# One stage for the front of block 1: projection, convolution, decay and scan on a ring of weight slabs

## The chip, the cores and the metric

The kernel runs on one core of a Trainium2 chip. It is one launch, and its time is the device time of that launch in microseconds. Of the core's engines, TensorE (PE in the profile) multiplies, with its weight loads shown apart (PEld); VectorE (DVE), ScalarE (ACT) and GpSimd (POOL) work element by element; SyncE (SP) issues the DMAs. Each engine takes its instructions strictly in the order in which they are written, and waits on semaphores where an operand comes from another engine.

## What is computed

Two blocks of two layers each work on a sequence of 512 positions and 1024 channels in float32. The change touches the front of block 1:

```
h = rms_norm(x, g_mix[i])
(a_q, a_k, a_v, s_z, s_x, s_b, s_c, s_dtf, s_dtb,
 c_q, c_k, c_v, d_uv) = jnp.split(h @ w_in[i], offsets, axis=-1)        # 2824 columns
...
xbc = jax.nn.silu(depthwise_conv_centred(jnp.concatenate([xs, bm, cm], axis=-1), conv_w, conv_b))
delta_f = jax.nn.softplus(dt_f.astype(f32) + dtb_f.astype(f32))
y_f = ssd_chunked(xh, delta_f, -jnp.exp(alog_f.astype(f32)), bg, cg)
y_b = jnp.flip(ssd_chunked(jnp.flip(xh, 1), jnp.flip(delta_b, 1), ...), 1)
y = (y_f + y_b + d_skip[:, None] * xh).reshape(b, s, d_x) * jax.nn.silu(z)
return rms_norm(y, g_norm)
```

`ssd_chunked` is a scan in four chunks of 128 positions, for four heads and in two directions: cumulated decays, their exponentials (`decay_in`), the products of C and B within a chunk (here "gram"), a state per chunk (`chunk_states`), the states carried from chunk to chunk, and the outputs. Behind the front stand two attentions, a spatial gate, the branch gates and `w_out`, then a mixture of experts and a gated side input.

## The kernel before

A product "exact" in float32 is made of three fast ones: both operands are split into a high part (ScalarE rounds it, `ring_hi`, `W_hi`, `T_hi`) and a low part (VectorE subtracts, `ring_lo`, `W_lo`, `T_lo`), and TensorE adds hi x hi, lo x hi and hi x lo. Every weight therefore passes DMA, ScalarE and VectorE before TensorE can use it. A float32 product without the split stands in the program once and in the trace as two records.

A layer of block 1 is a row of stages. Each is one `nc.Block()`: all engines meet at its end.

- `norm_stage`: norms the residual `X`, transposes it, and leaves `T_hi` and `T_lo`, channels on the partitions. With `save` it also writes `X` to DRAM (2 MB). Its parameter `slabs` (block 2 uses it) loads three weight slabs and splits the first.
- `project_stage`: 2824 columns in six chunks of 472, each for four token tiles and in two halves of the contraction, 24 products a tile, 576 in all. A half chunk of weights is loaded when `lo_ready` says its buffer is split. ScalarE and VectorE evict into `Z`, tokens on the partitions. The skewed bias table is written meanwhile.
- `conv_stage`: transposes the x, B and C channels to have channels on the partitions (24 transposes), convolves over five taps (VectorE, L544 and L549), applies silu with a sigmoid table, and transposes four tiles back (16).
- `decay_stage`: softplus, cumulative sums by products with triangular matrices (L601, L602), `spread` tiles (L629), their column sums over all partitions (L607), the differences (L641), exponentials (ScalarE, L592), and a product on GpSimd (L614).
- `scan_stage`: gram products (L687), diagonal outputs (L693), states (L697), `prev` carried by VectorE (L745 to L751), outputs (L706), gate and norm (L758 to L778).
- `late_stage`: 32 gate tiles, the two attentions and `w_out`, in an order that `steps` and `order` write out. Gate weights come in slabs of 1 MB through a ring of three (`ring_land`): slab q + 3 is requested when the last step of slab q is done (`load_slab`), then split by `to_hi` and `to_lo`. Four `turn` steps (j == 8 and j == 10) transpose the second attention's q and k tiles out of `Z` into `QK`.

The order on every engine is the order of the code; there is no scheduler.

## Time and profile before

| | |
|---|---|
| median of 3 runs | 4164.09 us (4161.66 to 4168.14) |
| the profiled execution | 4161.74 us, its span 4160.0 us |
| mean granted TensorE clock | 0.936 of full speed |
| busy: PE, DVE, ACT, POOL | 3607.9, 1716.3, 1080.5, 24.3 us |
| DMA | 644.75 MB, mean 155 GB/s |

How to read it: the span runs from the first to the last instruction; the rest of an execution's time lies around it. Shares of the whole span mix stages with different limits, so the change is read from the stages it touches. A row of the timeline is a run of like instructions: start, length, engine, line, operation, names of what is written and read, and in brackets how long the engine had been idle and whose work ended that. Overlapping TensorE records have modelled ends: the distance of starts tells their pace. In a stretch's row, "PEclk" is the granted clock, 1.00 being 2.4 GHz and 0.50 being 1.2 GHz.

### The profile page before, as it was taken

The numbers are of one execution on the slowest core, as the hardware profiler recorded it, in microseconds if no ns is written. First come the engines' busy times: TensorE is split into PE (matmuls) and PEld (weight loads), VectorE is DVE, ScalarE is ACT, GpSimd is POOL, SyncE is SP. The second block draws the span as 40 slices with busy tenths as digits, with TensorE's granted clock in tenths as the row PEclk, the third lists the DMA queues.
The fourth block names the chain that finished last, engine by engine and source line by source line (L and its number), as shares of the span: only waits on it lengthen the run. The fifth ranks groups of instructions, "written<-read, shape, count | busy, mean of one in ns | idle before, by whom it ended". The sixth has DMA issues, their size and how long they took to land. (4 is left out here: it accounts for less than half of the span.)

```text
span 4160.0 us, 45410 instructions
## 1 busy us (share of the span) xinstructions
PE 3607.9 (87%) x17600; PEld 2423.6 (58%) x17600; DVE 1716.3 (41%) x3020; ACT 1080.5 (26%) x1655; POOL 24.3 (1%) x34
## 2 busy tenths in 40 slices
PE   7669996999988679996999975989899869898998
PEld 6546675444457456674444453756666746566666
DVE  2475643212133565643221232347643323486433
ACT  3233321100123223321101033333332133323321
POOL 0010000000000000000000000000000000000000
PEclk9879998999998879998999998989999989899999
DMA  3121125999923121125999914111112241111122
GB/s 134 49 89 51 64 89 210 423 424 424 423 91 114 40 98 55 51 89 244 423 424 423 423 67 192 61 41 51 58 70 76 95 174 61 41 51 66 61 76 102
DMA packets 128280, 644.75 MB, mean 155 GB/s; under 512 B 19749, under 2 KB 42277, under 8 KB 61785
## 3 DMA queue, kind: packets, MB, share of 16 engines
q1 hardware_dynamic: 128088, 642.17, 39.3%
q8 instruction: 124, 2.03, 0.2%
q14 instruction: 68, 0.55, 0.0%
HBM read 631.61 MB, written 14.70 MB: 155 GB/s over the span
## 5 line engine op out<-in xcount | busy, mean ns | idle before, releaser
L1463 PE MATMUL ps<-normed_T_hi,ring_split 128*128 128x512 f32 (+1 forms) x1952 | 638.0, 409 | 42.1 <-PEq L268 15.6
L1463 PEld LDWEIGHTS ps<-normed_T_hi,ring_split 128*128 128x128 f32 (+1 forms) x1952 | 369.5, 193 | 155.1 <-issue 45.8
L1463 PE MATMUL ps<-normed_T_lo,ring_split 128*128 128x512 f32 (+1 forms) x976 | 387.7, 397 | 0.0
L2112 PE MATMUL ps<-normed_T_hi,ring_split 128*128 128x512 f32 x1024 | 338.1, 412 | 18.1 <-DVE branches L2371 16.1
L1739 DVE TENSOR_TENSOR ring_split<-weight_ring,ring_split 128x2048 fp32r<-128x2048 f32 x76 | 174.0, 2290 | 300.9 <-ACT ring_split L1624 300.9
L2112 PEld LDWEIGHTS ps<-normed_T_hi,ring_split 128*128 128x128 f32 x1024 | 194.1, 193 | 89.9 <-issue 29.7
L257 PE MATMUL ps<-weights_hi,normed_T_hi 128*128 128x472 f32 (+1 forms) x512 | 199.0, 389 | 32.2 <-DVE weights_lo L361 23.3
L1463 PEld LDWEIGHTS ps<-normed_T_lo,ring_split 128*128 128x128 f32 (+1 forms) x976 | 187.4, 192 | 42.4
L2112 PE MATMUL ps<-normed_T_lo,ring_split 128*128 128x512 f32 x512 | 203.5, 397 | 0.0
L257 PE MATMUL ps<-weights_lo,normed_T_hi 128*128 128x472 f32 (+1 forms) x512 | 197.6, 386 | 0.0
L257 PE MATMUL ps<-weights_hi,normed_T_lo 128*128 128x472 f32 (+1 forms) x512 | 196.4, 384 | 0.0
L1519 PE MATMUL ps<-branches 128*128 128x512 f32 x384 | 173.0, 593 | 1.6 <-DVE work L1813 1.6
L1036 PE MATMUL ps<-weight_ring,projected 128*64 128x512 f32 x768 | 167.9, 593 | 0.0
L1624 ACT ACTIVATE ring_split<-weight_ring 128x2048 fp32r<-128x2048 f32 x76 | 144.7, 1907 | 36.3 <-DMA weight_ring<-in_w_slabs 28.2
L2155 PE MATMUL ps<-branches,rope_tables_T 128*128 128x512 f32 x256 | 121.3, 596 | 9.4 <-DVE work L2356 5.2
L1014 PEld LDWEIGHTS ps<-work,projected 128*128 128x128 f32 x1024 | 119.1, 197 | 14.9 <-issue 14.9
L257 PEld LDWEIGHTS ps<-weights_hi,normed_T_hi 128*128 128x128 f32 x512 | 98.3, 192 | 48.9 <-issue 33.5
L1701 ACT ACTIVATE work<-work,small 128x256 f32<-128x256 f32 (+3 forms) x128 | 65.8, 514 | 233.6 <-DVE small L1887 115.4
L1111 DVE SCALAR_TENSOR_TENSOR result_lo<-ps,small,result_hi 128x1024 fp32r<-128x1024 f32 x16 | 20.5, 1283 | 255.9 <-ACT result_hi L1086 255.9
L1014 PE MATMUL ps<-work,projected 128*128 128x128 f32 x1024 | 122.0, 282 | 3.4 <-PEq L898 3.4
L2334 DVE TENSOR_TENSOR ring_split<-weight_ring,ring_split 128x2048 fp32r<-128x2048 f32 x40 | 91.7, 2291 | 78.9 <-ACT ring_split L2228 77.4
L361 DVE TENSOR_TENSOR weights_lo<-weight_ring,weights_hi 128x1888 fp32r<-128x1888 f32 (+1 forms) x30 | 64.8, 2159 | 143.0 <-ACT weights_hi L356 143.0
(399 smaller groups left out, 6056.0 us busy)
## 6 DMA issues: line engine op xcount, KB each, us to landing
weight_ring<-in_w_slabs SPq DMA_DIRECT2D x78, 1024.0 KB, 4.8
weight_ring<-in_w_exp_gate SPq DMA_DIRECT2D x48, 1024.0 KB, 16.6
weight_ring<-in_w_exp_down SPq DMA_DIRECT2D x48, 1024.0 KB, 12.5
weight_ring<-in_w_exp_up SPq DMA_DIRECT2D x48, 1024.0 KB, 20.8
weight_ring<-in_w_branch_gate SPq DMA_DIRECT2D x32, 1024.0 KB, 4.8
spare_weights<-in_w_exp_up SPq DMA_DIRECT2D x32, 1024.0 KB, 21.2
spare_weights<-in_w_exp_gate SPq DMA_DIRECT2D x32, 1024.0 KB, 20.3
spare_weights<-in_w_exp_down SPq DMA_DIRECT2D x32, 1024.0 KB, 16.0
```

The lines of the kernel that those rows point to most:

```text
L257: ins = e.matmul(dst, x[:, 4 * kh + k, t * P:(t + 1) * P], w[:, k, :], start=kh == 0 and k == 0 and m == 0, stop=kh == halves - 1 and k == ...
L361: e.tensor_tensor(W_lo[:, kh, 0:n], landing[:, kh, 0:n], W_hi[:, kh, 0:n].bitcast(F32), ALU.subtract).then_inc(s["lo_ready"], 1)
L1014: ins = e.matmul(PS[:, 6 + k // 4, (k % 4) * P:(k % 4 + 1) * P], U[:, t, k * P:(k + 1) * P], chosen[:, t, :], start=t == 0, stop=t == NT - 1)
L1036: ins = e.matmul(PS[64 * ex:64 * ex + 64, 2 * mat + half, :], lhs[:, 4 * kh + k, 64 * ex:64 * ex + 64], ring[u % 8][ex][:, k, :], start=kh ...
L1463: ins = e.matmul(dst, lhs(k, m), rhs(k, m), start=k == 0 and m == 0, stop=k == KD - 1 and m == 2)
L1519: ins = e.matmul(PS[:, 7, :], side[:, g % 2, k, :], BRT2[:, 4 * n + k, :], start=k == 0, stop=k == 3)
L1624: e.activation(ring_hi[:, q % 3, :], ring_land[:, q % 3, :], ACT.Copy).then_inc(s["slab_hi"], 1)
L1701: e.activation(Pr[:, u % 4, 0:n], Sl[:, u % 4, 0:n], ACT.Exp, bias=nmax[:, u:u + 1], accum_out=rsum[:, u:u + 1]).then_inc(s["exp_done"], 1)
L1739: e.tensor_tensor(ring_lo[:, q % 3, :], ring_land[:, q % 3, :], ring_hi[:, q % 3, :].bitcast(F32), ALU.subtract).then_inc(s["slab_lo"], 1)
L2112: ins = e.matmul(dst, lhs(k, m), rhs(k, m), start=k == 0 and m == 0, stop=k == KD - 1 and m == 2)
L2155: ins = e.matmul(PS[:, 7, :], side[:, q % 2, k, P * st["half"]:P * st["half"] + P], BRT[:, 2 * n + k, :], start=k == 0, stop=k == 1)
L2334: e.tensor_tensor(ring_lo[:, q % 3, :], ring_land[:, q % 3, :], ring_hi[:, q % 3, :].bitcast(F32), ALU.subtract).then_inc(s["slab_lo"], 1)
```

## The change

The four stages between the first norm and `late_stage` become one, `front_stage`.

- The weights `w_in` are laid out anew as `w_front`, 11 slabs of 1 MB for the ring of three that block 2 and `late_stage` use, and `w_dt`, the eight decay columns. Slabs 0 to 2 hold the 768 channels of x, B and C, slabs 9 and 10 the q and k of the second attention. These tiles have the weights as the stationary operand, so they come out with channels on the partitions. Slabs 3 to 8 are three pairs of halves for 512 token columns each. Every tile is 512 wide.
- The norm before it requests slabs 0 to 2 and splits slab 0; the loads and the save of `X` now stand ahead of the slabs in `norm_stage`, in block 2 too.
- The parts of the convolution, decay and scan stand between the dense tiles on TensorE, and between the slab splits on ScalarE and VectorE. Silu is made of tanh. ScalarE makes all 22 evictions. GpSimd adds the two directions' decay tiles, which VectorE did.
- The last stretch of the front requests the first three slabs of `late_stage`. Its four turns go.

The core of the diff (long lines are moved to the left):

```diff
         if slabs is not None:
             for q in range(3):
                 e.dma_start(ring_land[:, q, :], slabs(q)).then_inc(slot_loaded[q] if q else s["slab_landed_0"], 16)
-        for dst, src in loads:
-            e.dma_start(dst, src).then_inc(s["inputs_loaded"], 16)
         if experts_of is not None:
...
         if save:
-            e.dma_start(x_saved.rearrange("(t p) d -> p t d", p=P), X[:, :, :]).then_inc(s["stored"], 16)
             e.wait_ge(s["stored"], 16)
...
-def project_stage(w_dram, col0, chunks, width, total=None):
...
-def conv_stage(l):
...
-def decay_stage(l):
...
-def scan_stage(l):
...
+        e.dma_start(ssm_row, a["ssm_row"][l, :].partition_broadcast(P)).then_inc(s["inputs_loaded"], 16)
+        for q in range(3, FRONT_SLABS):
+            e.wait_ge(s["dense_ready"], last_step(q - 3) + 1)
+            e.dma_start(ring_land[:, q % 3, :], a["w_front"][l, q, :, :]).then_inc(landed[q % 3], 16)
+        for h in range(4):
+            e.dma_start(skew[h:h + 1, :].rearrange("a (p c) -> (a p) c", p=P)[:, 0:1024], bias_rows[h, :].partition_broadcast(P)).then_inc(s["side_landed"], 16)
+        for q in (2, 0, 1):
+            e.wait_ge(s["dense_ready"], last_step(8 + (q + 1) % 3) + 1)
+            e.dma_start(ring_land[:, q, :], late_slab(l, q)).then_inc(slot_loaded[3 + q], 16)
+        e.wait_ge(s["side_landed"], 64)
...
+    @block.tensor
+    def _(e):
+        def channels(q, h):
+            o = tile_of(q, h)
+            if q:
+                e.wait_ge(s["slab_lo"], q)
+            if o >= 4:
+                e.wait_ge(s["dense_scalar"], o - 3)
...
+            for k in range(KD):
+                for m, (w, x) in enumerate(((hi, T_hi), (lo, T_hi), (hi, T_lo))):
+                    ins = e.matmul(PS[:, o % 4, :], w[:, k, :], x[:, k, :], start=k == 0 and m == 0, stop=k == KD - 1 and m == 2)
+            ins.then_inc(s["dense_ready"], 1)
...
+        def steps_of_dt():
+            e.wait_ge(s["lo_ready"], 1)
+            for t in range(NT):
+                for k in range(KD):
+                    for m, (x, w) in enumerate(((T_hi, dt_hi), (T_hi, dt_lo), (T_lo, dt_hi))):
+                        ins = e.matmul(PS[:, 7, t * 8:(t + 1) * 8], x[:, k, t * P:(t + 1) * P], w[:, k, :], start=k == 0 and m == 0, stop=k == KD - 1 and m == 2)
+            ins.then_inc(s["side_ready"], 1)
...
+        def rows_of(i):
+            e.wait_ge(s["stage_d"], i + 1)
+            if i >= 3:
+                e.wait_ge(s["stage_f"], i - 3 if i > 3 else 1)
+            e.matmul(PS[:, 4 + (i + 1) % 4, :], ones, spread[:, i % 4, :, :], start=True, stop=True).then_inc(s["stage_g"], 1)
+        def turn_tokens(t):
+            e.wait_ge(s["xc_ready"], 4)
+            e.wait_ge(s["stage_f"], 8)
+            for c in range(4):
...
+        def gram(t):
+            if t < 2:
+                e.wait_ge(s["xc_ready"], 6)
+                e.wait_ge(s["turned_taken_scalar"], t + 1)
+            else:
+                e.wait_ge(s["gram_used"], t - 1)
...
+        def outputs(t):
+            b = 4 + 2 * (t % 2)
+            e.wait_ge(s["product_taken"], 1)
+            if t >= 2:
+                e.wait_ge(s["output_taken"], t - 1)
...
+        channels(0, 0)
+        steps_of_dt()
+        channels(0, 1)
+        channels(1, 0)
+        cumulated()
+        rows_of(0)
+        rows_of(1)
+        channels(1, 1)
+        rows_of(2)
+        rows_of(3)
+        channels(2, 0)
+        rows_of(4)
+        rows_of(5)
+        channels(2, 1)
+        rows_of(6)
+        rows_of(7)
+        for t in range(NT):
+            tokens(3, t)
+        tokens(4, 0)
+        for t in range(NT):
+            turn_tokens(t)
+        tokens(4, 1)
+        tokens(4, 2)
+        gram(0)
+        gram(1)
+        tokens(4, 3)
+        gram(2)
+        tokens(5, 0)
+        gram(3)
+        for t in range(1, NT):
+            tokens(5, t)
+            states(t - 1)
+        tokens(6, 0)
+        states(3)
+        tokens(6, 1)
+        tokens(6, 2)
+        outputs(0)
+        outputs(1)
+        tokens(6, 3)
+        tokens(7, 0)
+        outputs(2)
+        tokens(7, 1)
+        outputs(3)
+        tokens(7, 2)
+        tokens(7, 3)
+        for t in range(NT):
+            tokens(8, t)
+        for q in (9, 10):
+            for h in range(2):
+                channels(q, h)

+        def to_hi(q):
+            if q < 3:
+                e.wait_ge(slot_loaded[q], 16)
+            else:
+                e.wait_ge(landed[q % 3], 16 * ((q - 3) // 3 + 1))
+            e.activation(ring_hi[:, q % 3, :], ring_land[:, q % 3, :], ACT.Copy).then_inc(s["slab_hi"], 1)
+        def evict(o):
+            e.wait_ge(s["dense_ready"], step_of_tile(o) + 1)
...
+        def decay_exp(i):
+            d, t = pairs[i]
+            v = decay[:, d, t, :, :]
+            e.wait_ge(s["stage_f"], i + 1)
+            e.activation(v, v, ACT.Exp).then_inc(s["stage_h"], 1)
...
+        to_hi(1)
+        to_hi(2)
+        e.wait_ge(s["inputs_loaded"], 48)
         e.activation(ea, alog, ACT.Exp).then_inc(s["scalar_step"], st.add("scalar_step"))
+        evict(0)
...
+        evict(1)
+        evict(2)
+        to_hi(3)
+        tanh(0)
+        tanh(1)
+        evict(3)
+        for i in range(4):
+            decay_exp(i)
+        evict(4)
+        to_hi(4)
+        tanh(2)
+        tanh(3)
+        evict(5)
+        for i in range(4, 8):
+            decay_exp(i)
...
+        to_hi(5)
+        tanh(4)
+        tanh(5)
+        evict(6)
+        for t in range(NT):
+            take_tokens(t)
+        evict(7)
+        evict(8)
+        to_hi(6)
+        evict(9)
+        e.wait_ge(s["dense_scalar"], 10)
+        e.activation(zs, Z[:, :, Z_Z:Z_Z + 256], ACT.Tanh).then_inc(s["gate_ready"], 1)
+        to_hi(7)
...
+        to_hi(10)
+        for o in range(14, 22):
+            evict(o)
...
+        for i, (d, t) in enumerate(pairs):
+            v = decay[:, d, t, :, :]
+            e.wait_ge(s["stage_h"], i + 1)
+            e.tensor_tensor(v, v, delta[:, t, 4 * d:4 * d + 4].unsqueeze(2).to_broadcast([P, 4, P]), ALU.mult).then_inc(s["stage_done"], 1)
+            if d:
+                both = decay[:, 0, t, :, :]
+                e.wait_ge(s["stage_done"], i + 1)
+                e.tensor_tensor(both, both, v, ALU.add).then_inc(s["pool_ready"], 1)
...
+        def to_lo(q):
+            e.wait_ge(s["slab_hi"], q)
+            e.tensor_tensor(ring_lo[:, q % 3, :], ring_land[:, q % 3, :], ring_hi[:, q % 3, :].bitcast(F32), ALU.subtract).then_inc(s["slab_lo"], 1)
...
+            last = 0 if d else P - 1
+            e.wait_ge(s["stage_g"], i + 1)
+            inner(e.tensor_copy(r_last[:, d, t, :], rows[:, :, last]))
+            for h in range(4):
+                ins = e.scalar_tensor_tensor(decay[:, d, t, h, :], rows[:, h, :], acs[:, d, t, h:h + 1], neg_ge if d else neg_le, ALU.subtract, ALU.add)
+                if h < 3:
+                    inner(ins)
+            ins.then_inc(s["stage_f"], 1)
...
+        def conv(c0):
+            e.wait_ge(s["dense_scalar"], c0 + 2)
...
-        e.wait_ge(s["stage_e"], 2)
+        for i in range(4):
+            spread_of(i)
+        e.wait_ge(s["pool_ready"], 2)
+        conv(0)
+        e.wait_ge(s["stage_e"], 1)
+            inner(e.tensor_copy(acs[:, d, :, :], PS[:, 4, 16 * d:16 * d + 16].rearrange("p (t h) -> p t h", t=NT)))
+        after_inner()
+        to_lo(3)
+        for i in range(2):
+            take_rows(i)
+            spread_of(i + 4)
+        silu(0)
+        silu(1)
+        for i in range(2, 4):
+            take_rows(i)
+            spread_of(i + 4)
+        conv(2)
+        to_lo(4)
+        take_rows(4)
+        take_rows(5)
+        silu(2)
+        silu(3)
+        take_rows(6)
+        take_rows(7)
+        after_inner()
+        e.tensor_tensor(to_end, r_last, acs, ALU.subtract).then_inc(s["max_ready"], 1)
+        conv(4)
+        to_lo(5)
+        silu(4)
+        silu(5)
...
+            e.wait_ge(s["turned_taken_scalar"], t + 1)
+            scale_to_end(t)
+        use_gram(0)
+        use_gram(1)
+        to_lo(6)
+        use_gram(2)
+        use_gram(3)
+        e.wait_ge(s["gate_ready"], 1)
+        inner(e.scalar_tensor_tensor(zs, zs, 1.0, Z[:, :, Z_Z:Z_Z + 256], ALU.add, ALU.mult))
+        to_lo(7)
+        carry()
+        take_output(0)
+        to_lo(8)
+        for t in range(1, NT):
+            take_output(t)
...
+def late_slab(l, q):
+return a["w_branch_gate"][l, 4 * late_branch[q // 4] + q % 4, :, :] if q < 16 else a["w_out"][l, q - 16, :, :]
...
-    if j == 8:
-        turn(("cq", 0), C_Q, QK[:, 3, :], "S")
-        turn(("ck", 0), C_K, QK[:, 0, :], "V")
-    if j == 10:
-        turn(("cq", 1), C_Q + P, QK[:, 1, :], "S")
-        turn(("ck", 1), C_K + P, QK[:, 2, :], "V")
...
+jobs += [dict(p=p, t=t, hh=hh, q=Z[:, p, C_Q:C_Q + 512], k=Z[:, 2 + p, C_Q:C_Q + 512], keys=()) for p in range(2) for t in range(NT) for hh in range(2)]
...
-        load_slab(0)
+            e.dma_start(ring_land[:, q % 3, :], late_slab(l, q)).then_inc(landed[q % 3], 16)
         load_side(0)
-        load_slab(1)
         e.dma_start(ws, a["w_spatial"][l, :, :, :].rearrange("g t n -> t g n")).then_inc(s["stored"], 16)
-        load_slab(2)
...
         def to_hi(q):
-            e.wait_ge(landed[q % 3], 16 * (q // 3 + 1))
+            if q < 3:
+                e.wait_ge(slot_loaded[3 + q], 16)
+            else:
+                e.wait_ge(landed[q % 3], 16 * (q // 3))
...
-norm_stage([(gain_col, columns("g_mix", l))], gain_col, save=True)
-project_stage(a["w_in"][l, :, :], 0, 6, 472, IN1)
-conv_stage(l)
-decay_stage(l)
-scan_stage(l)
+norm_stage([(gain_col, columns("g_mix", l)), (dt_land, a["w_dt"][l, :, :])], gain_col, save=True, slabs=lambda q: a["w_front"][l, q, :, :])
+front_stage(l)
 late_stage(l)
```

On TensorE before, the chain's products stand by themselves behind the projection (L204 the transposes of the convolution, L601 to L607 the decay, L687 to L706 the scan):

```order
L380 UNCONDITIONAL_BRANCH
L510 UNCONDITIONAL_BRANCH
L204 MATMUL ps<-constants,projected 128x128 x24
L204 MATMUL ps<-constants,weight_ring 128x128 x16
L502 UNCONDITIONAL_BRANCH
L598 UNCONDITIONAL_BRANCH
L601 MATMUL ps<-small,constants 128x16
L602 MATMUL ps<-small,constants 128x16
L607 MATMUL ps<-weight_ring,constants 128x512 x8
L570 UNCONDITIONAL_BRANCH
L681 UNCONDITIONAL_BRANCH
L687 MATMUL ps<-weight_ring 128x128 x8
```

Now the cumulative sums (L483, L484) and two of the row sums (L490) stand between two dense tiles (L458, three products for each of eight parts of the contraction):

```order
L458 MATMUL ps<-normed_T_hi,ring_split 128x512 x2
L458 MATMUL ps<-normed_T_lo,ring_split 128x512
L483 MATMUL ps<-small,constants 128x16
L484 MATMUL ps<-small,constants 128x16
L490 MATMUL ps<-work,constants 128x512 x2
L458 MATMUL ps<-normed_T_hi,ring_split 128x512 x2
```

The 24 transposes at the head are gone, and the eight row sums stand in four pairs, each behind a dense tile.

On VectorE before, all 24 taps of the convolution (L549) run in one piece, and the decay's operations behind them:

```order
L544 TENSOR_SCALAR weight_ring<-weight_ring,small 128x512 x6
L549 SCALAR_TENSOR_TENSOR weight_ring<-weight_ring,small 128x512 x24
L554 TENSOR_TENSOR weight_ring<-weight_ring,work 128x512 x6
L557 COPY work<-ps 128x512 x2
L502 UNCONDITIONAL_BRANCH
L616 UNCONDITIONAL_BRANCH
L620 TENSOR_TENSOR small<-projected,small 128x32
```

Now, from the first spread tiles (L732) to the first two decay tiles (L742), with a third of the convolution (L750, L754) and the split of slab 3 (L726) between them:

```order
L732 TENSOR_TENSOR work<-constants,small 128x512 x4
L750 TENSOR_SCALAR branches<-branches,small 128x512 x2
L754 SCALAR_TENSOR_TENSOR branches<-branches,small 128x512 x8
L830 COPY small<-ps 128x16 x2
L726 TENSOR_TENSOR ring_split<-weight_ring,ring_split 128x2048
L740 COPY small<-ps 128x4
L742 SCALAR_TENSOR_TENSOR residual<-ps,small,constants 128x128 x4
L732 TENSOR_TENSOR work<-constants,small 128x512
L740 COPY small<-ps 128x4
L742 SCALAR_TENSOR_TENSOR residual<-ps,small,constants 128x128 x4
```

The first decay tile, which the fourth row sum on TensorE waits for, has moved behind the first third of the convolution and behind a slab split.

## Rows read from the trace of the kernel before

**Rows 1.** By stage: PE, PEld, DVE, ACT, POOL busy (records), PEclk, DMA share, GB/s.

```profile
36.30:163.20 126.90, 126.31 (x576) 110.66 (x576) 31.01 (x23) 24.85 (x23) 0.00 (x0) 0.98 0.29 93
163.20:252.70 89.50, 33.16 (x164) 25.59 (x164) 67.64 (x158) 24.17 (x42) 11.61 (x14) 0.65 0.01 2
```

**Rows 2.** Timeline: start, us, engine, line, operation [idle before it <- releaser].

```profile
13.90 0.38 SPq L285 DMA_DIRECT2D residual_scratch<-residual  x1
...
20.95 5.68 DVE L240 SCALAR_TENSOR_TENSOR normed_T_lo<-ps,small,normed_T_hi 128x512 fp32r<-128x512 f32 x8 [2.76 <-ACT normed_T_hi L234]
...
36.38 0.76 PE L257 MATMUL ps<-weights_hi,normed_T_hi 128*128 128x472 f32 x1 [11.66 <-DVE weights_lo L361]
...
170.72 16.37 DVE L549 SCALAR_TENSOR_TENSOR weight_ring<-weight_ring,small 128x512 f32<-128x512 f32 x24
...
200.55 0.19 DVE L620 TENSOR_TENSOR small<-projected,small 128x32 f32<-128x32 f32 x1 [5.40 <-DMA small<-in_a_log_b]
...
203.37 4.91 DVE L629 TENSOR_TENSOR weight_ring<-constants,small 128x512 f32<-128x512 f32 x8
...
258.02 1.91 ACT L2228 ACTIVATE ring_split<-weight_ring 128x2048 fp32r<-128x2048 f32 x1 [7.59 <-DMA weight_ring<-in_w_branch_gate]
...
259.96 2.29 DVE L2334 TENSOR_TENSOR ring_split<-weight_ring,ring_split 128x2048 fp32r<-128x2048 f32 x1 [7.61 <-ACT ring_split L2228]
...
262.91 1.22 PE L2112 MATMUL ps<-normed_T_hi,ring_split 128*128 128x512 f32 x2 [8.09 <-DVE branches L2371]
...
1257.35 6.27 DVE L240 SCALAR_TENSOR_TENSOR normed_T_lo<-ps,small,normed_T_hi 128x512 fp32r<-128x512 f32 x8 [2.77 <-ACT normed_T_hi L234]
...
1501.68 1.22 PE L2112 MATMUL ps<-normed_T_hi,ring_split 128*128 128x512 f32 x2 [8.00 <-DVE branches L2371]
```

**Rows 3.** By stretch: the projection's first 6 us, and its rest.

```profile
36.30:42.40 6.10, 6.02 (x15) 5.13 (x16) 2.12 (x1) 0.23 (x1) 0.00 (x0) 0.50 0.80 271
42.40:162.70 120.30, 120.28 (x562) 105.54 (x560) 28.41 (x21) 24.62 (x22) 0.00 (x0) 1.00 0.27 85
```

**Rows 4.** Timeline of TensorE: products 512 wide, 18 starts apart.

```profile
1219.72 0.39 PE L257 MATMUL ps<-weights_hi,normed_T_lo 128*128 128x512 f32 x1
...
1223.80 0.40 PE L257 MATMUL ps<-weights_hi,normed_T_lo 128*128 128x512 f32 x1
```

**Rows 5.** Timeline of TensorE: float32 products and transposes.

```profile
229.19 1.11 PE L697 MATMUL ps<-weight_ring,work 128*128 128x128 f32 x8
...
230.13 1.00 PE L693 MATMUL ps<-work,weight_ring 128*128 128x64 f32 x8
...
337.54 1.88 PE L2155 MATMUL ps<-branches,rope_tables_T 128*128 128x512 f32 x4
...
339.25 1.04 PE L2167 MATMUL ps<-constants,work 128*128 128x128 f32 x8
...
710.14 0.95 PE L1025 MATMUL ps<-small,work 128*128 x8
```

**Rows 6.** By stretch: products one column wide.

```profile
2533.00:2536.70 3.70, 3.70 (x31) 3.64 (x30) 3.08 (x5) 0.00 (x0) 0.00 (x0) 0.67 0.00 1
```

**Rows 7.** Timeline of VectorE and GpSimd in the scan.

```profile
220.43 0.75 DVE L734 TENSOR_TENSOR weight_ring<-work,small 128x256 f32<-128x256 f32 x2
...
223.86 3.14 POOL L713 TENSOR_TENSOR work<-work,small 128x256 f32<-128x256 f32 x4 [4.69 <-DMA work<-in_g_ssm]
...
224.95 1.58 DVE L734 TENSOR_TENSOR weight_ring<-work,small 128x256 f32<-128x256 f32 x2
```

**Rows 8.** DMA issues: name, queue, count, KB each, median us to landing.

```profile
residual_scratch<-residual SPq DMA_DIRECT2D x4, 2048.0 KB, 10.5
...
weight_ring<-in_w_in SPq DMA_DIRECT2D x24, 944.0 KB, 4.8
```

**Rows 9.** Timeline: the start of a layer of block 2.

```profile
2555.37 2.28 DVE L339 TENSOR_TENSOR ring_split<-weight_ring,ring_split 128x2048 fp32r<-128x2048 f32 x1
...
2557.97 1.19 PE L1463 MATMUL ps<-normed_T_hi,ring_split 128*128 128x512 f32 x2 [7.91 <-PEq L268]
```

582 lines of the change are left out of this document (248 added, 334 removed).

## Prediction

> **What bounds the kernel now.** I read the stretches first, because the change touches only the front of block 1, once in each of two layers. In [rows 1] the first layer is cut at the end of its projection. In the projection (36.3 to 163.2 us) TensorE is busy 126.3 of 126.9 us. In the three stages behind it, the convolution, the decay and the scan, 163.2 to 252.7, TensorE has 33.2 us of work in 89.5 us, and its mean granted clock is 0.65. VectorE has 67.6 us there and ScalarE 24.2: VectorE leads, but ScalarE and waits take turns with it. So each layer has 127 us bound by TensorE and then 90 us bound by a chain of small steps, with nothing dense beside it.
>
> The timeline then gives the edges [rows 2]. The last product of the norm (VectorE, L240) ends at 20.95 + 5.68 = 26.63. The first product of the projection starts at 36.38: the weights are requested only after the norm, and are then split by ScalarE and VectorE. At the other end ScalarE waits 7.59 us for the gate weights, splits them (1.91 us), VectorE makes the low part (2.29 us), and the first gate product starts at 262.91. From 26.63 to 262.91 are 236.3 us. In the second layer the same two events stand at 1257.35 + 6.27 = 1263.62 and 1501.68: 238.1 us. These two stretches, 474.4 us, are what the change rewrites.
>
> **The prices.** Dense products, 472 columns wide: 562 in 120.3 us at full clock, 0.214 us each; the first 6.1 us of a layer ran at clock 0.50 [rows 3]. Products 512 wide: 18 starts apart from 1219.72 to 1223.80, 0.2267 us each [rows 4]. A float32 product of 512 columns stands in the trace as two records; the four records at 337.54 last until the next operation starts at 339.25, so 0.43 us a record; the eight transposes at 339.25 take 1.04 us, some 0.12 each as one record [rows 5]. Records of float32 products 128 or 64 wide are 0.94 us for eight (229.19 to 230.13), and those with one or two columns 0.95 us for eight: 0.12 us, however narrow [rows 5].
>
> **The front stage, part by part, for one layer.** Its TensorE work in order of size:
> - Dense: 11 slabs, each 48 products for a channel slab or for half the contraction of 512 token columns, 528 in all of 512 columns. 528 x 0.2267 = 119.7 us, against 576 x 0.214 = 123.3 before. The first 6 us at half clock remain (TensorE still pauses over the splits): + 3.0, half of 6.1.
> - The eight decay columns are no longer part of a wide product. They take 96 products 8 columns wide, which no row shows in this number format. From above: the 0.12 us of the narrow float32 records, 11.5 us. From below: 0.2267 for 512 columns less the slope of the two widths, (0.2267 - 0.214)/40 a column, gives 0.07 us for 8, 6.4 us; the slope is taken over a short stretch, so I go down to 1.5 us. I take 11.5, the nearest row.
> - Row sums of the decay: 8 float32 products of 512 columns, 16 records x 0.43 = 6.8 us; the cumulative sums 4 records, 0.5 us.
> - Transposes: the 24 of the x, B and C channels go, since these channels are now computed transposed; 16 remain, 16 x 0.12 = 1.9 us.
> - Gram products, states and outputs: 8 + 12 + 28 = 48 products, 96 records x 0.11 = 10.6 us (four products with unused results are dropped).
> Sum 119.7 + 3.0 + 11.5 + 6.8 + 0.5 + 1.9 + 10.6 = 154.0 us. This becomes the length of the stage if the other engines keep up.
>
> **Do they keep up?** VectorE: 67.6 us of chain [rows 1], less the four evictions and copies it loses, plus ten slab splits of 2.29 us [rows 2], 22.9: about 88 of 154. ScalarE: ten splits of 1.91, 22 evictions at the price of a convolution tap (16.37 / 24 = 0.68 [rows 2]), and its part of the chain, 24.2 [rows 1], together 58. In sum nobody is near TensorE; what counts is the order, since every queue is in order. The tight joint is the fourth row sum: it may only overwrite its PSUM bank when VectorE has finished the first decay tile. Counted from the end of the narrow products, D: softplus 2.9 (2.8 lie between the VectorE rows at 200.55 and 203.37 [rows 2]), four spreads of 4.91 / 8 = 0.6, first pair of convolution channels (a third of the 16.4 us in [rows 2] and of the first taps, 6.4, but not before the second dense tile is evicted at D + 6.2) to D + 12.7, the sums copied, the split of slab 3 (ScalarE has it at D + 13.6) to D + 16.0, first decay tile D + 17.1. TensorE asks at: three dense tiles of 5.44 = 16.3, sums 0.5 and three rows 2.6, D + 19.4. So 2.3 us of slack. Walked on in the same way, the low part of slab 4 is ready at D + 33 and wanted at D + 45, the silu of the last channels at D + 49 and wanted at D + 55, slab 6 some 10 us early. The slabs themselves: slot q is free after slab q - 3, a slab computes for 11 us, and the landing takes 4.8 us [rows 8] plus 4.2 of splits, against 22 us until it is wanted. TensorE meets what it asks for at nearly every joint; I add 2 us for queue turns: 156.0.
>
> **A term against the change.** GpSimd now multiplies and adds decay tiles while VectorE runs the convolution. In [rows 7] two VectorE products of 128x256 that took 0.75 us together at 220.43 took 1.58 at 224.95, while GpSimd worked (223.86 to 227.00) on the same kind. The Trainium skill ("SBUF — State Buffer", section "SBUF: two separate sides") says that the port pair the two share is held for a whole instruction and that the other blocks; the trace agrees, with +0.83 us. GpSimd has 16 operations in the new stage; at the 11.61 / 14 = 0.83 us of [rows 1] that is 13 us, so with some margin at most 15 us of VectorE time per layer. With 66 us of slack on VectorE most of it is covered; what is not falls on the joint at D + 55 (6 us of slack, 8 operations before it), which could be 2 us late. It stays in the bound.
>
> **The edges.** Slab 0 is loaded and split within the norm. Block 2 already does this: VectorE ends its split at 2555.37 + 2.28 and TensorE starts at 2557.97, 0.3 us later [rows 9]. In block 1 the 2 MB save of the residual now stands ahead of the slab. It was requested at 13.90 [rows 2] and lands after 10.5 us [rows 8], at 24.4; slab 0 shares the queues with it, and by my estimate lands some 2 us behind it, 26.4. Splits 1.9 + 2.3: ready at 30.6, 4.0 us after the norm, against 9.8 before. If it lands while the norm still runs, it is 3.4; if it starts only behind the save, 4.8 us for 1 MB [rows 8], it is 6.8. Block 2's norms get the same order; [rows 9] shows no slack behind the split there, so a later landing would be seen; I estimate nothing, at most 1 us a layer. At the far end the three gate slabs are in place: last eviction 0.7, stage change 0.5 (an estimate), splits 1.9 + 2.3, one copy 0.7, that is 6.1 us to the first gate product instead of the 10.2 from 252.70 [rows 1] to 262.91. In the gate stage four steps that turned the attention's q and k go, 16 transposes: 2.0 us, if TensorE leads there, and 0 if not.
>
> **The sum.** Per layer 4.0 + 156.0 + 6.1 = 166.1. Saved: 236.3 + 238.1 - 2 x 166.1 = 142.2, plus 2 x 2.0 = 146.2. The profiled execution took 4161.74 us (span 4160.0 and 1.7 around it); less 146.2 is 4015.5. The median of the runs is 2.3 us above that execution; I forecast 4016.
>
> **Rivals.**
> 1. The narrow products cost less. At 1.5 us in place of 11.5 the result is 4016 - 20 = 3996. For it: the slope above. Against it: every narrow record of the trace costs 0.11 to 0.12. The Trainium skill ("TensorE: Matmul & The Clock Gate", section "Back-to-back issue gap") gives about 60 cycles, 25 ns, for 1 to 64 columns, but the same page's "LDWEIGHTS" has 128 columns of weights at 107 ns; by the first the 96 cost 2.4 us and the kernel comes to an estimated 3998, by the second 10.3 and 4014. No run here shows which holds for this format.
> 2. The narrow products cost the clock. At 2533.0 to 2536.7 TensorE ran 31 records one column wide and the granted clock was 0.67 [rows 6], so it fell to its lower level while the engine was busy. If it falls in the new stretch of 96, they cost twice 0.11, 0.22 each, 21.1 us, and the next dense products run at half clock for nearly as long as the first ones in [rows 3], + 2.4: + 12.0 per layer, 4040. Against it: other narrow stretches (eight of 128 and 64 columns) came at full speed.
> 3. VectorE comes late. If all of the 15 us of collisions met the tight joints, after their 2.3 and 6 us of slack, some 9 us per layer would be left: 4034; joined with rival 2, 4058.
> 4. Slower than before. The chain's products stand in the same in-order queue as the dense ones. If TensorE stopped at each of some 20 joints, the clock would stay low, as in the old chain (mean 0.65 [rows 1]). The point from which this decides: the stage would have to be 74 us longer per layer (148 / 2), 48% of its 154 at half clock (or as many waits). All of it at half clock gives 166 + 151 = 317 per layer (the 154 doubled, less the 3.0 already in it), 4016 + 302 = 4318. Against it: the walk above has the operands ready 2 to 12 us early, and the dense pieces between joints are 2.7 to 5.4 us of full work.
> 5. The change does not do what it says, if the stage change still waits for a load: each wait is at most the 7.6 us seen in [rows 2], 4 places, 4046.
>
> **How the numbers follow.** Forecast 62%, rival 1 15%, rival 2 11%, rival 3 7%, rival 5 2%, rival 4 3%. The range reaches from rival 1 to rival 2 and half of 3, 3994 to 4050. Within 0.2% of before (8.3 us, about what the measurement can tell) or slower needs a loss of nearly all 146 us: slower 3%, same 1%, faster 96%.
>
> **What would show it.** In the new profile: first dense product 3.4 to 4.5 us after the norm's last L240-like operation; TensorE above 95% busy from there to the last dense tile, some 156 us, at clock 1.0 but for the first 6 us; the 96 narrow records in 11 to 12 us (6 or less: rival 1; above 15 with a clock below 1: rival 2); TensorE idle before the row sums or the gram products with a VectorE releaser: rival 3; the first gate product 6 us after the last dense one. Wrong outright if TensorE is under 80% busy in the stage.

## The result, and the profile after

The changed kernel takes 4020.1 us (median of 4 runs, 4018.6 to 4023.6), against 4164.8 us for the kernel before in the same runs: a ratio of 0.965, with a 95% interval of 0.964 to 0.966. The forecast was 4016 us, the range 3994 to 4050. The profiled execution has a span of 4016.8 us, 143.2 less than the 4160.0 before; 146.2 was the forecast.

The timeline of the changed kernel has the same edges as [rows 2]: the end of the norm, ScalarE's split of slab 0, the first product of the front, the first gate product, and the first gate product of the second layer.

```profile
21.26 5.68 DVE L229 SCALAR_TENSOR_TENSOR normed_T_lo<-ps,small,normed_T_hi 128x512 fp32r<-128x512 f32 x8 [2.77 <-ACT normed_T_hi L223]
...
25.70 1.93 ACT L303 ACTIVATE ring_split<-weight_ring 128x2048 fp32r<-128x2048 f32 x1
...
30.27 1.19 PE L458 MATMUL ps<-normed_T_hi,ring_split 128*128 128x512 f32 x2 [5.26 <-PEq L257]
...
198.66 1.22 PE L2212 MATMUL ps<-normed_T_hi,ring_split 128*128 128x512 f32 x2 [3.81 <-DVE branches L2474]
...
1362.65 1.22 PE L2212 MATMUL ps<-normed_T_hi,ring_split 128*128 128x512 f32 x2 [3.81 <-DVE branches L2474]
```

The norm ends at 21.26 + 5.68 = 26.94. From there to the first gate product are 171.7 us, against 236.3 in [rows 2]; in the second layer 171.8 (from 1190.89) against 238.1. ScalarE splits slab 0 at 25.70 with no wait for its load. Between the edges the stretches answer to [rows 1] and [rows 3] (busy time and records of PE, PEld, DVE, ACT and POOL, then PEclk, DMA share, GB/s):

```profile
30.30:36.50 6.20, 6.20 (x15) 4.86 (x16) 4.38 (x3) 5.31 (x5) 0.09 (x2) 0.53 0.11 26
38.60:42.90 4.30, 4.30 (x41) 4.30 (x39) 0.00 (x0) 0.60 (x1) 0.00 (x0) 1.00 0.01 4
42.90:54.90 12.00, 12.00 (x58) 12.00 (x59) 0.00 (x0) 0.00 (x0) 0.00 (x0) 0.50 0.00 0
54.90:60.10 5.20, 5.20 (x13) 4.12 (x14) 2.82 (x7) 1.97 (x4) 0.00 (x0) 0.51 0.00 0
60.10:192.60 132.50, 132.09 (x625) 108.04 (x623) 81.17 (x147) 43.23 (x65) 18.55 (x16) 1.00 0.28 96
30.27:192.63 162.36, 161.94 (x756) 135.05 (x756) 88.80 (x157) 51.13 (x75) 18.67 (x18) 0.93 0.23 79
```

The last row is the whole stage: TensorE is busy 161.94 of 162.36 us, where it was busy 33 of 90 us behind the old projection. The 89 us of VectorE and 51 of ScalarE lie beside it. What TensorE waited for, in that stretch, is two rows long (what waited and for whom: us in total, times, longest us); the first is the wait before the stage:

```profile
PE ps L458 <- PEq L257: 5.3, 1, 5.3
PE ps L506 <- DVE residual L776: 0.4, 1, 0.4
```

So the chain fits between the dense products almost without a gap. What is left to see is in rows two to four of the table: the narrow products. Their timeline at the start, where the pace changes, and at the end:

```profile
38.58 0.17 PE L478 MATMUL ps<-dt_hi,normed_T_hi 128*128 128x8 f32 x1
...
42.74 0.25 PE L478 MATMUL ps<-dt_hi,normed_T_lo 128*128 128x8 f32 x1
42.85 0.28 PE L478 MATMUL ps<-dt_hi,normed_T_hi 128*128 128x8 f32 x1
42.99 0.35 PE L478 MATMUL ps<-dt_lo,normed_T_hi 128*128 128x8 f32 x1
43.21 0.35 PE L478 MATMUL ps<-dt_hi,normed_T_lo 128*128 128x8 f32 x1
...
54.94 1.20 PE L458 MATMUL ps<-normed_T_hi,ring_split 128*128 128x512 f32 x2
```

Their starts are 0.111 us apart until 42.9 and 0.213 us apart after it: the granted clock fell from 2.4 to 1.2 GHz (1.00 to 0.50) with TensorE busy all the time. The second layer shows the same, with 39 products at the faster pace. The 96 took 16.4 us, and the next dense tile ran its first 12 products at half clock, 5.2 us instead of 2.7.

**Where the 143.2 us are.** The stretch from the norm's end to the first gate product gave 64.6 + 66.3 = 130.9. From there to the first product of `w_out` the gate stage gave 3.9 and 3.8 (336.2 us in both layers before, 332.3 and 332.4 after). Behind that, up to the next norm's end or the first product of block 2, it is 4.6 and 2.5 less, block 2 is 2.2 longer, and the start 0.3. VectorE waits for the reload of the residual there, which lands after 7.8 and 8.0 us in place of 8.9 and 9.4; that explains 1.1 and 1.4 us of the two. The rest is no larger than the scatter: from the first `w_out` product to the next layer's first product the other kernels of this study that leave that code and the norm's alone took 663.3 to 666.9 us, and the changed kernel's profile has 663.3, at their lower end.

### The profile page after: what moved, and what is told of

Its sections match the earlier page's. It is cut to its first block and busy times, and to the rows that moved or that the text cites. A ratio compares the mean times of both kernels' runs of the same rounds, so it can differ in the third digit from the quotient of the medians.

```text
span 4016.8 us, 45112 instructions
## 1 busy us (share of the span) xinstructions
PE 3608.9 (90%) x17600; PEld 2411.1 (60%) x17600; DVE 1693.3 (42%) x2970; ACT 1080.5 (27%) x1673; POOL 38.6 (1%) x42
## 5 line engine op out<-in xcount | busy, mean ns | idle before, releaser
L2212 PE MATMUL ps<-normed_T_hi,ring_split 128*128 128x512 f32 x1024 | 340.0, 414 | 9.2 <-DVE branches L2474 7.6
L1119 PEld LDWEIGHTS ps<-work,projected 128*128 128x128 f32 x1024 | 119.1, 197 | 14.9 <-issue 14.9
L470 PE MATMUL ps<-ring_split,normed_T_hi 128*128 128x512 f32 x384 | 121.3, 397 | 0.0
L458 PE MATMUL ps<-normed_T_hi,ring_split 128*128 128x512 f32 x320 | 109.3, 425 | 10.5 <-PEq L257 10.5
L1624 PEld LDWEIGHTS ps<-branches 128*128 128x128 f32 x384 | 72.2, 189 | 76.1 <-issue 72.2
L1568 PE MATMUL ps<-ring_split,normed_T_hi 128*128 128x256 f32 x512 | 99.8, 296 | 19.9 <-DVE projected L1874 13.0
L1141 PEld LDWEIGHTS ps<-weight_ring,projected 128*64 128x64 f32 x768 | 54.4, 137 | 105.2 <-issue 105.1
```

What stands on the lines that cost most here:

```text
L458: ins = e.matmul(PS[:, o % 4, :], w[:, k, :], x[:, k, :], start=k == 0 and m == 0, stop=k == KD - 1 and m == 2)
L470: ins = e.matmul(PS[:, o % 4, :], x[:, 4 * kh + k, t * P:(t + 1) * P], w[:, k, :], start=kh == 0 and k == 0 and m == 0, stop=kh == 1 and k ...
L1119: ins = e.matmul(PS[:, 6 + k // 4, (k % 4) * P:(k % 4 + 1) * P], U[:, t, k * P:(k + 1) * P], chosen[:, t, :], start=t == 0, stop=t == NT - 1)
L1141: ins = e.matmul(PS[64 * ex:64 * ex + 64, 2 * mat + half, :], lhs[:, 4 * kh + k, 64 * ex:64 * ex + 64], ring[u % 8][ex][:, k, :], start=kh ...
L1568: ins = e.matmul(dst, lhs(k, m), rhs(k, m), start=k == 0 and m == 0, stop=k == KD - 1 and m == 2)
L1624: ins = e.matmul(PS[:, 7, :], side[:, g % 2, k, :], BRT2[:, 4 * n + k, :], start=k == 0, stop=k == 3)
```

## The experiments

All medians are to be read beside 4020.1 for the changed kernel, and the quoted text in each experiment is what was expected before it ran. The kernel before, run beside them, had medians of 4164.7 to 4166.2. "Front" is the time from the first product behind the norm to the first gate product, 168.4 us in both layers of the changed kernel. "Theory" and "rival" are the explanations that an experiment was to decide between.

**1. Chain parts behind the dense part.** The three lists of calls are reordered: all dense tiles first, then `cumulated`, the row sums, the turns, gram, states and outputs; the same on ScalarE and VectorE.

```diff
-        cumulated()
-        rows_of(0)
-        rows_of(1)
         channels(1, 1)
...
         for q in (9, 10):
             for h in range(2):
                 channels(q, h)
+        cumulated()
+        for i in range(8):
+            rows_of(i)
```

> Same stage, same operations, but the convolution, decay and scan parts stand behind all dense tiles on TensorE, ScalarE and VectorE. Theory, the gain is the overlap: TensorE's 137 us without the chain, then a chain led by VectorE's 66 us and its waits, 75 to 90 us, so 217 instead of 162 us a layer, 4020 + 110 = 4130. Rival, most of the gain comes from cheaper pieces (no transposes of 24 tiles, fewer stage ends, wider products): at most 4060.

Measured: 4118.5 us (ratio to before 0.989, 0.987 to 0.990). The front takes 214.6 and 215.4 us, 46.2 and 47.0 more. The two stretches of the first layer, and TensorE's longest waits in the second of them:

```profile
30.84:172.00 141.16, 141.16 (x629) 119.62 (x630) 32.35 (x29) 35.13 (x43) 0.11 (x2) 0.92 0.27 91
172.00:245.39 73.39, 31.20 (x137) 23.75 (x136) 60.44 (x131) 18.83 (x35) 17.75 (x16) 0.66 0.08 25
```

```profile
PE ps L496 <- DVE residual L713: 12.3, 1, 12.3
PE ps L2193 <- PEq L430: 7.9, 1, 7.9
PE ps L506 <- DVE branches L733: 7.5, 1, 7.5
```

The second row looks like the 89.50 us of [rows 1]: VectorE leads with 60 us, and the clock is at 0.66. So of 130.9 us gained in the fronts, 93 are the overlap. The other 38 are what is left: this kernel keeps one stage instead of four, loads before their stage, 512-wide tiles, and no transposes of the x, B and C channels. Only the loads have a run of their own (experiment 6), for the gate slabs. The time is 98 us above the changed kernel where the theory had 110, and the rival, at most 4060, falls.

**2. Narrow products mixed with dense ones.** Four of the 96 stand behind each of the 24 products of the second tile.

```diff
-        steps_of_dt()
-        channels(0, 1)
+        for k in range(KD):
+            for m, (w, x) in enumerate(((hi, T_hi), (lo, T_hi), (hi, T_lo))):
+                ins = e.matmul(PS[:, 1, :], w[:, k, :], x[:, k, :], start=k == 0 and m == 0, stop=k == KD - 1 and m == 2)
+                for t, kk, mm in narrow[4 * (3 * k + m):4 * (3 * k + m) + 4]:
+                    xx, ww = ((T_hi, dt_hi), (T_hi, dt_lo), (T_lo, dt_hi))[mm]
+                    last = e.matmul(PS[:, 7, t * 8:(t + 1) * 8], xx[:, kk, t * P:(t + 1) * P], ww[:, kk, :], start=kk == 0 and mm == 0, stop=kk == KD - 1 and mm == 2)
```

> The 96 narrow decay products are spread between the 24 products of the second dense tile, four behind each. In the changed kernel they run in one piece: 39 at 0.111 us, then the granted clock falls and 57 take 0.213, and the next dense products run 5.1 us at half clock (2.4 us lost). Theory, the clock falls because nothing but narrow products runs for 16 us: mixed, they cost 96 x 0.111 = 10.7 instead of 16.4, and the 2.4 us are saved, 8.1 us a layer: 4020.1 - 16.2 = 4004. Rival, narrow products lower the clock however they are mixed: 4020 or more.

Measured: 4029.3 us, and the front is 3.1 and 3.0 us longer. The theory fell, and the rival's 4020 or more came. Up to and behind the fall of the clock:

```profile
37.28:43.40 6.12, 6.12 (x47) 5.71 (x46) 0.00 (x0) 0.60 (x1) 0.00 (x0) 1.00 0.01 3
43.40:62.60 19.20, 19.20 (x77) 17.77 (x77) 0.13 (x1) 0.00 (x0) 0.00 (x0) 0.50 0.00 0
```

At full clock a third of the mixture's time is dense products (0.227 of 0.67 us), and the clock fell all the same, and then these dense products ran at half clock too. Other mixtures were not tried.

**3. A third of the narrow products.**

```diff
-        for m, (x, w) in enumerate(((T_hi, dt_hi), (T_hi, dt_lo), (T_lo, dt_hi))):
-            ins = e.matmul(PS[:, 7, t * 8:(t + 1) * 8], x[:, k, t * P:(t + 1) * P], w[:, k, :], start=k == 0 and m == 0, stop=k == KD - 1 and m == 2)
+        ins = e.matmul(PS[:, 7, t * 8:(t + 1) * 8], T_hi[:, k, t * P:(t + 1) * P], dt_hi[:, k, :], start=k == 0, stop=k == KD - 1)
```

> Of the three products for each part of the decay columns only high by high is made: 32 narrow products in place of 96, all else in its place. It leaves out the low parts of the decay columns. In the changed kernel 39 of the 96 ran at 0.111 us before the clock fell. Theory, the clock falls only when the narrow piece goes on beyond that: 32 x 0.111 = 3.6 us at full clock, and the next dense tile at full clock, less 16.4 - 3.6 + 2.4 = 15.2 us a layer, 4020.1 - 30.4 = 3990. Rival, the fall belongs to this place or to what comes behind and stays: 12.8 or less a layer, 3994.5 or more.

Measured: 3993.2 us, the front 13.6 and 13.3 us shorter: 15.2 was the theory, 12.8 the rival's most. In the trace the narrow piece and what follows it:

```profile
38.10:41.60 3.50, 3.50 (x34) 3.50 (x32) 0.00 (x0) 0.60 (x1) 0.00 (x0) 1.00 0.02 5
41.60:42.80 1.20, 1.20 (x7) 0.97 (x7) 0.19 (x1) 0.76 (x3) 0.00 (x0) 0.89 0.00 0
42.80:47.60 4.80, 4.80 (x16) 3.81 (x15) 2.88 (x6) 1.21 (x2) 0.00 (x0) 0.67 0.00 0
```

In this layer the 32 ran at full clock, as the theory had it. But the clock fell behind them, over dense products, which show no fall in experiment 4, where no narrow piece stands before them. In the second layer it fell within the last of the 32, and 5.7 us of dense products ran at 0.50. The fall comes late and is paid by whatever stands there then. That is the part of the rival that held; the time lies between the two forecasts.

**4. The decay columns as the stationary operand.** 24 products 512 wide at the head of the stage, a copy of 8 partitions, four small transposes.

```diff
-        ins = e.matmul(PS[:, 7, t * 8:(t + 1) * 8], x[:, k, t * P:(t + 1) * P], w[:, k, :], start=k == 0 and m == 0, stop=k == KD - 1 and m == 2)
+        ins = e.matmul(PS[0:8, 7, :], w[:, k, :], x[:, k, :], start=k == 0 and m == 0, stop=k == KD - 1 and m == 2)
...
+    def turn_dt():
+        for t in range(NT):
+            ins = e.transpose(PS[:, 6, t * 8:(t + 1) * 8], T[0:8, t * P:(t + 1) * P], ident[0:8, 0:8])
```

> The decay columns become the stationary operand: 24 products of 512 columns in place of 96 of 8, at the head of the stage, then a copy of 8 partitions by ScalarE and four small transposes behind the first dense tile. Theory, a product's price is its moving columns and its load, so few wide ones are cheap and keep the clock: 24 x 0.227 + 4 x 0.12 = 5.9 us in place of 16.4 + 2.4, less 12.8 us a layer, 4020.1 - 25.7 = 3994. Rival, a stationary operand of 8 columns is slow or lets the clock fall: above 4004.

Measured: 3993.6 us (ratio to before 0.959, 0.958 to 0.960), the front 14.3 and 13.7 us shorter.

```profile
30.56:36.60 6.04, 6.04 (x21) 2.14 (x22) 4.46 (x3) 5.04 (x4) 0.00 (x0) 0.77 0.10 26
36.60:178.60 142.00, 141.60 (x669) 115.38 (x666) 84.29 (x155) 46.36 (x71) 18.55 (x16) 1.00 0.27 90
```

Behind the start there is no fall any more: one row of 142 us at clock 1.00. The narrow products and the clock that they cost are worth 16.4 + 2.5 - 5.9 = 13.0 us of this, the theory's 12.8. The rest, 1.3 and 0.7 us, lies at the start of the stage: over its first 6.1 us the clock is 0.77 and 0.67 in the two layers, and 0.52 in both of the changed kernel. That is not an effect of the edit alone: in experiment 2, whose first tile is unchanged, it is 0.75.

**5. The turns put back.** The four `turn` steps of the second attention stand in the gate stage again.

```diff
         for j in range(3, 28):
+            if j == 8:
+                turn(("cq", 0), C_Q, QK[:, 3, :], "S")
+                turn(("ck", 0), C_K, QK[:, 0, :], "V")
```

> The four turns of the second attention stand in the gate stage again, where they stood (their results are not used). The changed kernel is 8.5 and 6.3 us faster behind its front, where 2.0 us a layer were forecast for the turns. Theory one, all of that hangs on the turns (their copies by ScalarE and VectorE, and waits, too): 4020 + 13 = 4033 or more. Theory two, the turns are worth the 2.0 us of their transposes and the rest comes from other causes (the reload of the residual lands 1.2 us sooner, the clock comes back at other places): 4024.

Measured: 4028.3 us. The gate stage takes 336.1 and 336.4 us, within 0.2 us of the kernel before, so the turns are worth 3.8 and 3.9 us a layer; what lies behind it stayed within its scatter. Theory one fell, since the rest does not hang on the turns, and theory two had the price too low. The second pair, at j == 10:

```profile
322.14 0.66 PE L2234 MATMUL ps<-constants,projected 128*128 128x128 f32 x4
324.13 0.66 PE L2234 MATMUL ps<-constants,projected 128*128 128x128 f32 x4 [1.34 <-ACT work L2357]
```

Between the two turns TensorE waits 1.34 us for ScalarE. Two PSUM banks take turns there, so the second turn needs the bank of the step before the first; a turn is so short that ScalarE has not yet read that bank (L2357).

**6. The gate slabs requested late again.**

```diff
-        for q in (2, 0, 1):
-            e.wait_ge(s["dense_ready"], last_step(8 + (q + 1) % 3) + 1)
-            e.dma_start(ring_land[:, q, :], late_slab(l, q)).then_inc(slot_loaded[3 + q], 16)
...
+        load_slab(0)
```

> The first three gate slabs are requested in the gate stage again instead of in the last stretch of the front. Theory, they are worth the wait they removed: last dense product to first gate product 6.0 us now, 10.2 before, so + 4.2 a layer, 4020 + 8.4 = 4028.5. Rival, the wait was hidden by something else: 4020.

Measured: 4031.6 us, the front 5.9 and 4.9 us longer, where the theory had 4.2. ScalarE's wait in the new stage, and TensorE's:

```profile
199.28 1.91 ACT L2331 ACTIVATE ring_split<-weight_ring 128x2048 fp32r<-128x2048 f32 x1 [6.24 <-DMA weight_ring<-in_w_branch_gate]
```

```profile
204.17 1.22 PE L2212 MATMUL ps<-normed_T_hi,ring_split 128*128 128x512 f32 x2 [9.76 <-DVE branches L2474]
```

The loads that now start ahead of the stage are worth 11.5 us in the two layers; the rival, 4020, fell.

**7. The save behind the slabs.** In `norm_stage` the two requests change places, as they stood in the kernel before.

```diff
-        if save:
-            e.dma_start(x_saved.rearrange("(t p) d -> p t d", p=P), X[:, :, :]).then_inc(s["stored"], 16)
         if slabs is not None:
             for q in range(3):
                 e.dma_start(ring_land[:, q, :], slabs(q)).then_inc(slot_loaded[q] if q else s["slab_landed_0"], 16)
+        if save:
+            e.dma_start(x_saved.rearrange("(t p) d -> p t d", p=P), X[:, :, :]).then_inc(s["stored"], 16)
```

> In the norm the 2 MB save of the residual is requested behind the three slabs, as before the change; all else stays. In the changed kernel ScalarE splits slab 0 with no wait, 3.3 us from norm to first product. Theory, slab 0 is early in either order: 4020, within 2 us. Rival, the order matters: behind the slabs it frees slab 0 sooner (4018 or less), or it makes a later stage wait for the save to end (4024 or more).

Measured: 4019.5 us, no difference in the median. ScalarE splits slab 0 without a wait here too. The save now lands 14.8 us after its request instead of 7.7. The norm's stage cannot end before it, and in the second layer that shows: VectorE's split ends at 1195.03 and the first product starts 1.1 us later, where the changed kernel has 0.3.

```profile
1192.74 2.29 DVE L329 TENSOR_TENSOR ring_split<-weight_ring,ring_split 128x2048 fp32r<-128x2048 f32 x1 [0.80 <-ACT ring_split L303]
...
1196.16 1.19 PE L458 MATMUL ps<-normed_T_hi,ring_split 128*128 128x512 f32 x2 [6.16 <-PEq L257]
```

The save, requested at 1180.74, took 14.9 us, to 1195.6. So the part of the rival on a wait for the save holds, at 0.8 us in one layer, too little to see in the median.

**8. VectorE made late.** Twelve products of 128x256 stand ahead of the split of slab 3.

```diff
+        after_inner()
+        for _ in range(12):
+            e.wait_ge(s["vector_step"], st.counts["vector_step"])
+            inner(e.tensor_tensor(tmp, consts[:, 0:256], consts[:, 0:256], ALU.mult))
         after_inner()
         to_lo(3)
```

> VectorE makes 12 useless products of 128x256 (5 to 5.5 us, into a scratch tile) ahead of the split of slab 3 and the first decay tile. Theory, in in-order queues the slack of the tightest joint counts, not the 70 us that VectorE is idle in the stage: the fourth row sum had 2.4 us, so TensorE waits some 3 us a layer there, 4020 + 6 = 4026. Rival, the idle time absorbs it: 4020. Rival two, lateness is passed on from joint to joint and the clock falls: above 4030.

Measured: 4031.2 us (4027.0 to 4035.5), the front 4.1 and 4.2 us longer. VectorE's added work and the first decay tile, and TensorE's wait for that tile:

```profile
69.90 5.49 DVE L834 TENSOR_TENSOR work<-constants 128x256 f32<-128x256 f32 x12
...
77.76 1.12 DVE L742 SCALAR_TENSOR_TENSOR residual<-ps,small,constants 128x128 f32<-128x128 f32 x4
```

```profile
79.02 2.05 PE L490 MATMUL ps<-work,constants 128*128 128x512 f32 x2 [2.49 <-DVE residual L742]
```

The 5.5 us of work make the split of slab 3 start 4.9 us later, counted from the copies of the sums before it (69.54 to 75.48, against 70.02 to 71.04): in the changed kernel VectorE had stood idle 0.8 us ahead of it, for ScalarE's half of that slab. TensorE waits 2.5 us at this joint, so its slack is 2.4 us, as in the profile of the changed kernel. Of the 73 us that VectorE stands idle in the stage only those 0.8 helped. Two more losses follow. The third gram product waits 1.2 us in place of 0.4, and the granted clock is at half speed behind the wait of 2.5 us:

```profile
79.02:82.30 3.28, 3.28 (x6) 1.96 (x7) 3.28 (x9) 1.15 (x2) 2.02 (x2) 0.50 0.26 107
```

Half of these 3.3 us is lost, 1.6. The three losses make 4.9 us; the clock came back sooner at the start of the stage (0.69 over the first 6.1 us in place of 0.52, 1.0 us), which leaves about the 4.1 measured. The second layer has the same wait (2.4 us) and the same fall behind it. So the theory is right that the slack of the joint counts and not the idle time, but rival two came as well, with its fallen clock and its time above 4030: what a late joint costs is more than its wait.

**9. GpSimd's work made small.** This leaves out nearly all of the product with delta and of the sum of the two directions; GpSimd's twelve operations stay, on 128x8 elements each.

```diff
-        e.tensor_tensor(v, v, delta[:, t, 4 * d:4 * d + 4].unsqueeze(2).to_broadcast([P, 4, P]), ALU.mult).then_inc(s["stage_done"], 1)
+        e.tensor_tensor(v[:, :, 0:2], v[:, :, 0:2], delta[:, t, 4 * d:4 * d + 4].unsqueeze(2).to_broadcast([P, 4, 2]), ALU.mult).then_inc(s["stage_done"], 1)
```

> GpSimd's eight products and four sums on the decay tiles work on 2 of the 128 columns of each head; this leaves out the product with delta and the sum of the two directions in the other columns. In the changed kernel VectorE's operations beside them took longer: two silus 3.00 us in place of 1.28, two first taps 2.75 in place of 1.00, eight taps 7.20 in place of 5.38, in all 6.7 us up to 108.4 us. Theory, that is the collision with GpSimd, and it costs the kernel only the 0.4 us a layer that TensorE waits for VectorE: the durations come back to 1.28, 1.00 and 5.38, the time is 4019 to 4020. Rival one, the durations stay (something else slows them). Rival two, the collisions cost more than TensorE's waits show: 4014 or less.

Measured: 4021.7 us, no difference. In the changed kernel VectorE and GpSimd beside each other show:

```profile
93.09 1.04 POOL L704 TENSOR_TENSOR residual<-residual,small 128x512 f32<-128x512 f32 x1 [9.64 <-ACT residual L619]
...
93.37 3.00 DVE L762 SCALAR_TENSOR_TENSOR branches<-work,branches 128x512 f32<-128x512 f32 x2
...
94.21 1.62 POOL L708 TENSOR_TENSOR residual<-residual 128x512 f32<-128x512 f32 x1
...
98.61 2.75 DVE L750 TENSOR_SCALAR branches<-branches,small 128x512 f32<-128x512 f32 x2
101.29 7.20 DVE L754 SCALAR_TENSOR_TENSOR branches<-branches,small 128x512 f32<-128x512 f32 x8
```

and with small GpSimd work the same three, and one operation of GpSimd:

```profile
91.52 1.28 DVE L762 SCALAR_TENSOR_TENSOR branches<-work,branches 128x512 f32<-128x512 f32 x2
...
95.02 1.00 DVE L750 TENSOR_SCALAR branches<-branches,small 128x512 f32<-128x512 f32 x2
...
95.75 9.06 POOL L704 TENSOR_TENSOR residual<-residual,small 128x8 f32<-128x8 f32 x1 [0.58 <-ACT residual L619]
...
95.94 5.38 DVE L754 SCALAR_TENSOR_TENSOR branches<-branches,small 128x512 f32<-128x512 f32 x8
...
103.44 1.28 DVE L762 SCALAR_TENSOR_TENSOR branches<-work,branches 128x512 f32<-128x512 f32 x2
```

All three durations are back, and TensorE's 0.4 us of wait is gone: the collisions are real, some 7 us a layer, and lie under TensorE's work. They take slack all the same. The silu of the last channels ends 7.9 us before the first gram product starts here (104.7 and 112.6), and 1.1 us before it in the changed kernel (111.9 and 113.0).

**10. The first gate slab split in the front**, by ScalarE ahead of the last eviction and by VectorE behind slab 10.

```diff
         for o in range(14, 21):
             evict(o)
+        e.wait_ge(slot_loaded[3], 16)
+        e.activation(ring_hi[:, 0, :], ring_land[:, 0, :], ACT.Copy).then_inc(s["slab_hi"], 1)
+        evict(21)
```

> The first gate slab is split at the end of the front stage, by ScalarE ahead of the last eviction and by VectorE behind its last slab, instead of in the gate stage. Theory, the 6.0 us between the last dense product and the first gate product are the stage change (1.2), the first transposes (0.6) and a copy (0.7) once the splits (4.2) are gone, some 2.6 to 2.8: less 3.3 us a layer, 4020 - 6.6 = 4013.5. Rival, the new first thing is another load or copy of that stage: 4018 to 4020.

Measured: 4012.1 us, the front 3.2 and 3.0 us shorter. The theory had 4013.5. The first gate product follows the transposes almost at once:

```profile
193.97 1.07 PE L2234 MATMUL ps<-constants,projected 128*128 128x128 f32 x8 [1.01 <-PEq L430]
195.39 0.73 PE L2217 MATMUL ps<-normed_T_hi,ring_split 128*128 128x512 f32 x2 [0.35 <-DVE branches L2479]
```

**11. Experiments 4 and 10 together.**

> Both together: the wide decay products (-26.6 measured alone) and the first gate slab split in the front (-8.0 measured alone). They touch opposite ends of the stage. Theory, they add: 4020.1 - 34.6 = 3985.5. Rival, with the stage 14 us shorter a joint of the chain or a slab is late and takes some back: 3989 or more.

Measured: 3985.2 us (ratio to before 0.957, 0.956 to 0.958). They add, to 0.3 us; the rival, 3989 or more, did not come.

**12. And the wide decay products made in the norm.** Behind its transposes TensorE makes them while slab 0 is split.

```diff
+        e.wait_ge(s["stage_a"], 1)
+        for m, (x, w) in enumerate(((T_hi, dt[1]), (T_hi, dt[2]), (T_lo, dt[1]))):
+            for k in range(KD):
+                if m != 1:
+                    e.wait_ge(s["lo_ready" if m else "turned_taken_scalar"], k + 1)
+                e.matmul(PS[0:8, 7, :], w[:, k, :], x[:, k, :], start=k == 0 and m == 0, stop=k == KD - 1 and m == 2)
```

> As the one before, and the 24 wide decay products are made at the end of the norm, while TensorE waits for the split of slab 0 (5.7 us idle before the first product). Theory, they fill that wait and bring the clock up: they start near 25.0 instead of 30.6, their cold part lies where TensorE stood still, and the stage change comes some 3.5 us later: less 4 to 5 us a layer, 3985.5 - 9 = 3976. Rival, slabs 1 and 2 are split later by as much, since ScalarE and VectorE pass the stage change only behind TensorE, and the chain is late: 3982 or more.

Measured: 3972.0 us (3969.1 to 3975.1; ratio to before 0.954, 0.953 to 0.955), 48 us below the changed kernel and the fastest here. The decay products and the first dense ones of the front:

```profile
24.72 2.09 PE L352 MATMUL ps<-normed_T_hi,dt_hi 128*8 128x512 f32 x8
26.64 2.02 PE L352 MATMUL ps<-normed_T_hi,dt_lo 128*8 128x512 f32 x8
28.50 2.01 PE L352 MATMUL ps<-normed_T_lo,dt_hi 128*8 128x512 f32 x8
30.81 0.71 PE L470 MATMUL ps<-normed_T_hi,ring_split 128*128 128x512 f32 x2 [0.30 <-PEq L257]
```

The same two pieces by stretch:

```profile
24.72:30.40 5.68, 5.68 (x27) 2.10 (x25) 4.61 (x5) 3.10 (x4) 0.00 (x0) 1.00 0.53 225
30.81:36.60 5.79, 5.76 (x25) 4.44 (x25) 3.87 (x2) 5.70 (x6) 0.11 (x2) 1.00 0.12 28
```

They end within 0.4 us of VectorE's split (30.51 and 30.14), so the stage change comes no later than before, where the theory had it 3.5 us later. They run at clock 1.00 from the start, right behind the norm's transposes, and the front starts at 1.00 too, where experiment 11 has 0.77 and 0.68 over the first 6.1 us behind 5.7 us of waiting, and the changed kernel 0.52 behind 5.3. These two are why it gave 13.2 us and not the 9 forecast; the rival did not come.

## Why the prediction was right, and where its sizes were off

- **What bounds the front.** Right. The dense products set the length and the chain lies beside them; with the chain behind them 93 us are lost again (experiment 1). TensorE is busy 161.94 of the stage's 162.36 us, at clock 1.00 but for the start and the narrow products.
- **The stage, 156.0 us.** It took 162.4. Two terms of the sum were too small. The narrow products were 11.5 and came to 16.4. The clock that they cost the next tile, 2.5, stood only in rival 2. The 2 us kept for joints were 0.4. Together 4.9 + 2.5 - 1.6 = 5.8 of the 6.4 us.
- **Rival 2** is what happened, at part of its price: 7.4 us a layer instead of 12.0, because the first 39 products still ran at full clock. The forecast held against it that runs of "eight of 128 and 64 columns" in [rows 5] came at full speed, and took them as evidence for 96. [Rows 6], with 31 records and a fallen clock, were nearer to the case and got 11%. **Rival 1** was wrong for this format: 0.111 us each at full clock. Of the two rules of the Trainium skill ("TensorE: Matmul & The Clock Gate") weighed there, the trace bears out the 107 ns of "LDWEIGHTS" and not the 25 ns of "Back-to-back issue gap", a section that says itself that its gap for few columns leaves the weight load out.
- **The walk through the joints.** The fourth row sum was to have 2.3 us of slack. In the profile it has 2.4 (decay tile done at 74.4, TensorE there at 76.9), and experiment 8 gives 2.4 as well. The silu of the last channels was to have 6 us; it has 1.1, and 7.9 without the collisions of rival 3 (experiment 9). The third gram product waited 0.4.
- **Rival 3.** The collisions exist and cost VectorE some 7 of the 15 us allowed for. They cost the kernel nothing that can be measured (experiment 9), since they fell on the joint with the larger slack and used up nearly all of it.
- **The edges.** Near edge 3.3 for 4.0: slab 0 lands before ScalarE is free in either order of the requests (experiment 7), so the estimate of 26.4 for its landing was late. It rests on the 10.5 us of [rows 8], a median over four saves of two kinds: in the kernel before, the two of block 1 landed after 6.6 us each and the two of block 2 after 14.5 and 14.6. In the changed kernel the first save took 7.6. Far edge 6.0 for 6.1.
- **The turns.** 3.9 us a layer for 2.0: the term counted TensorE's transposes and not the waits around them, of which the trace shows one of 1.34 us (experiment 5).
- **The sum.** Fronts 11.3 us worse than forecast, turns 3.7 better. The other 4.6 us, which no term forecast, are what lies behind the gate stage less what block 2 and the start gave back: 2.5 of them the reload, the rest not above the scatter. That the sum came within 3 us of 143.2 is therefore partly luck: its largest error, 11.3, was offset by 3.7 + 4.6 = 8.3 from elsewhere.

## What to carry to other kernels

A chain of small steps is best hidden under an in-order queue of dense work, if each joint is walked for when its operand is ready and when it is asked for. Slack at the tightest joint counts, and idle time of the other engine hardly does; a joint that comes late can cost the clock behind the wait as well (experiment 8: a wait of 2.5 us, then 3.3 us at half clock). Products with few moving columns are dear twice, for their own time and for the clock of what follows; where the few columns can be the stationary operand, they cost what a few wide products cost (24 in place of 96 here). Useful work in TensorE's wait at a stage change also keeps its clock up.

## What the runs showed of the hardware that was not expected

- The clock fell from 1.00 to 0.50 (2.4 to 1.2 GHz) while TensorE was busy without a gap: within 96 narrow products, behind the first 39; within a mixture of narrow and dense ones; and behind a piece of 32 narrow ones, over dense products (experiment 3, first layer).
- Behind a wait of 2.5 us TensorE ran 3.3 us at clock 0.50 (experiment 8).
- A GpSimd operation on 128x8 elements, 0.20 us elsewhere, took 9.06 us beside VectorE's taps, slab split and silu, and ended when these did (104.81 and 104.72, experiment 9; the second layer has 9.06 too). GpSimd's spans are rough, but VectorE's work can hold up GpSimd as well as the other way round.
- A product with 8 stationary columns and 512 moving ones keeps the pace of one with 128 (runs of eight start 1.84 to 1.92 us apart in experiments 4 and 12; eight of the dense ones take 1.81) and did not lower the clock.
